# Recurrent heads: latent values and query computed as a fourth pair of half products

## The reference, cut to what matters

```
p = h @ w_in                       # q, zf, zb, i, g, b5, b6, b7, ... each 1024 wide
f = sigmoid(z); k = sigmoid(-z)    # per direction (with the zero lower bounds of one layer)
s_t = f_t * s_{t-1} + k_t v_t      # over context, then latent tokens; the other direction reversed
o_t = q_t s_t                      # only the latent tokens' outputs are used
a = rmsnorm(o_fwd + o_bwd) * silu(g)
b = p5 * conv3(p6 * p7)
```

## Time and profile before

| | |
|---|---|
| runs | 2821.94, 2821.27, 2818.16 us; median 2821.27 |
| span of the profiled execution | 2814.1 us, first to last instruction |
| TensorE busy | 2697.8 us (96%) |
| VectorE / ScalarE / GpSimd busy | 1246.7 (44%) / 523.0 (19%) / 171.2 (6%) us |
| mean granted TensorE clock | 0.987 of full speed |
| recurrent heads 1 to 7 | about 125 us to 665 us of the span |

### The profile page before, as it was taken

The page is one execution under the profiler, slowest core; times in us unless marked ns, Lnnn a source line. Parts: engine busy times, 40 slices in busy tenths (PEclk is TensorE's granted clock), DMA queues, the critical chain, the costliest instruction groups (busy, mean ns, idle before and its releaser), DMA issues.

```text
span 2814.1 us, 32083 instructions
## 1 busy us (share of the span) xinstructions
PE 2697.8 (96%) x12682; PEld 1796.7 (64%) x12682; DVE 1246.7 (44%) x2310; ACT 523.0 (19%) x870; POOL 171.2 (6%) x140
## 2 busy tenths in 40 slices
PE   7999999999899999999799999989999999999997
PEld 3688888887544444586344333334496877888886
DVE  4255656664444344535311111146573335654644
ACT  3122121222233233211100000022322113100001
POOL 1122211220000000132000000000000000000000
PEclk9999999999999999999899999999999999999999
DMA  9622111211111111225599999942102421233330
GB/s 346 212 60 57 54 52 45 60 30 38 38 53 53 45 53 49 79 75 183 231 409 409 409 409 409 409 154 64 42 1 83 125 77 46 78 87 90 90 90 30
DMA packets 327673, 374.57 MB, mean 133 GB/s; under 512 B 10033, under 2 KB 273030, under 8 KB 324230
## 3 DMA queue, kind: packets, MB, share of 16 engines
q1 hardware_dynamic: 327286, 371.93, 38.6%
q10 hardware_dynamic: 272, 1.05, 0.1%
HBM read 370.85 MB, written 2.10 MB: 133 GB/s over the span
## 4 chain that ended last, share of the span: by engine, by line
PE 91%; DVE 4%; DVEq 1%; DMA 1%; ACT 1%; issue 1%; SPq 0%; ACTq 0%
PE psum L1650 31%; PE psum L1952 12%; PE psum L1381 8%; PE psum L2108 6%; PE psum L720 3%; PE psum L1118 2%; PE psum L1837 2%; PE psum L815 2%; PE psum L728 2%; PE psum L2642 2%; PE psum L1878 2%; PE psum L705 2%; PE psum L1308 2%; PE psum L1360 2%; PE psum L1337 1%; PE psum L2724 1%
## 5 line engine op out<-in xcount | busy, mean ns | idle before, releaser
L1650 PE MATMUL psum<-arena 128*128 128x256 f32 x4144 | 907.9, 378 | 1.0 <-ACT arena L2740 0.5
L1650 PEld LDWEIGHTS psum<-arena 128*128 128x128 f32 x4144 | 779.2, 189 | 116.2 <-issue 5.3
L1952 PE MATMUL psum<-arena 128*64 128x512 f32 x1536 | 347.6, 597 | 3.0 <-issue 2.1
L1952 PEld LDWEIGHTS psum<-arena 128*64 128x64 f32 x1536 | 104.9, 136 | 217.5 <-issue 214.4
L1381 PE MATMUL psum<-arena 128*128 128x512 f32 x512 | 233.1, 597 | 0.0
L2108 PE MATMUL psum<-arena 128*128 128x512 f32 (+1 forms) x448 | 168.1, 532 | 0.0
L1682 DVE TENSOR_TENSOR arena<-psum,arena 128x256 f32<-128x256 f32 x66 | 28.0, 425 | 315.2 <-ACT arena L1695 192.6
L1381 PEld LDWEIGHTS psum<-arena 128*128 128x128 f32 x512 | 92.4, 189 | 104.1 <-issue 104.1
L1883 DVE SCALAR_TENSOR_TENSOR arena<-psum,arena 128x512 f32<-128x512 f32 x64 | 48.0, 750 | 246.4 <-PE psum L1878 245.8
L2108 PEld LDWEIGHTS psum<-arena 128*128 128x128 f32 x448 | 84.8, 190 | 80.8 <-issue 77.3
L1657 POOL TENSOR_TENSOR arena<-arena 128x512 f32<-128x512 f32 x34 | 48.2, 1418 | 1119.7 <-DMA arena<-in_w_in 653.3
(11 more groups left out here) (378 smaller groups left out, 3202.9 us busy)
## 6 DMA issues: line engine op xcount, KB each, us to landing
arena<-in_w_gate SPq DMA_DIRECT2D x64, 1024.0 KB, 18.3
arena<-in_w_up SPq DMA_DIRECT2D x64, 1024.0 KB, 16.2
arena<-in_w_down SPq DMA_DIRECT2D x64, 1024.0 KB, 18.0
arena<-in_w_in SPq DMA_DIRECT2D x120, 512.0 KB, 4.0
arena<-in_ada_w SPq DMA_DIRECT2D x24, 1024.0 KB, 7.4
arena<-in_w_up SPq DMA_DIRECT2D x32, 512.0 KB, 5.3
arena<-in_w_down SPq DMA_DIRECT2D x32, 512.0 KB, 4.8
arena<-in_w_out SPq DMA_DIRECT2D x16, 512.0 KB, 3.8
```

Of the source, the lines that this page charges most:

```text
L1650: mm = pe.matmul(psum[:, base + b, c * HALF:(c + 1) * HALF], w, v, start=(first and q == 0 and m in (0, 2, 3, 4)), stop=(last and q == KC ...
L1952: mm = pe.matmul(psum[64 * e:64 * e + 64, bank + n, :], tokens(e, 2 * q + k), w[:, k, 512 * n:512 * n + 512], start=(q == 0 and k == 0), s ...
```

## The change

Latent values and latent query become pair 3 of `pe_seven`. The values come out with channels on partitions, so TensorE turns them (four transposes) into bank 5, and ScalarE copies them straight into `hw_v`. Only the two context tiles keep the plain value product. The query stays in `hq_o` until `dve_take` has read it, and level 0 reads it there. The backward gates move behind pair 1, level 5 behind them; the values and key transposes stand ahead of pair 3; the states stand in the middle of pair 3; level 0 of the next head moves ahead of the head's norm sum. GpSimd forms four sums for a head. In head 0 the modulation parts stand elsewhere.

```diff
         def pool_hg_sums(pool, i, g):
 ...
             if g == 1 and not is_first(i):
-                done(pool, "hg", i - 1, 3)
+                done(pool, "hg", i - 1, 7)
             if g == 2:
                 if not is_first(i):
                     done(pool, "hg", i, 1)
                 pool.wait_ge(sem("head_gates"), i + 1)
+            if g == 3:
+                done(pool, "hg", i, 3)
             weight_sums(pool, *hg_pair(g), hg_sums(g), "hq_sums")
...
         def pe_hg_quad(pe, i, g, within):
-            pe.wait_ge(sem("hq_sums"), i * 3 + g)
-            pe.wait_ge(sem("hq_out"), i * 3 + g)
-            if g == 0:
-                pe.wait_ge(sem("head_query"), i)
+            pe.wait_ge(sem("hq_sums"), i * 4 + g)
+            pe.wait_ge(sem("hq_out"), i * 4 + g)
...
+        def pe_hg_gate(pe, i, d):
+            if d == 0 and not is_first(i):
+                pe.wait_ge(sem("head_out"), i)
+            ws.arrived(pe, "hg", i, 4 + d)
 ...
+            if d:
+                mm.then_inc(sem("head_gates"), 1)
...
+        def pe_turn_values(pe, i):
+            pe.wait_ge(sem("hq_out"), i * 4)
+            for t in range(LT):
+                mm = pe.transpose(psum[:, 5, t * P:(t + 1) * P], hq_o[:, t * P:(t + 1) * P], ident)
+            mm.then_inc(sem("head_turned"), 1)
...
         def dve_begin(dve, i):
-            dve.wait_ge(sem("head_query"), i)
-            dve.tensor_copy(hw_q0, hp_q)
+            dve.wait_ge(sem("head_forget"), i)
...
             pe_hg_quad(pe, 0, 1, lambda pe, q: late(6, 7) if q == 2 else None)
             late(8, 9)
-            pe_hg_values(pe, 0, 0)
-            late(10, 11)
-            pe_hg_quad(pe, 0, 2, lambda pe, q: late(12, 13) if q == 2 else None)
+            pe_hg_values(pe, 0)
+            pe_hg_quad(pe, 0, 2, lambda pe, q: late(10, 11) if q == 2 else None)
+            late(12, 13)
             late(14, 15)
-            pe_hg_values(pe, 0, 1)
-            pe_hg_query(pe, 0)
...
+            pe_hg_quad(pe, 0, 3, turn_first)
             pe_mod_turn(pe, 2)
+            pe_turn_values(pe, 1)
+            pe_level(pe, 1, 0)
...
-                pe_level(pe, i, 0)
                 pe_hg_quad(pe, i, 0, levels({3: 1}))
-                pe_hg_gates(pe, i, lambda: pe_level(pe, i, 2))
+                pe_hg_gate(pe, i, 0)
+                pe_level(pe, i, 2)
                 pe_hg_quad(pe, i, 1, levels({1: 3, 3: 4}))
+                pe_hg_gate(pe, i, 1)
                 pe_level(pe, i, 5)
-                pe_hg_values(pe, i, 0)
                 pe_hg_quad(pe, i, 2, levels({1: 6, 3: 7}))
-                pe.wait_ge(sem("head_values_out"), i * 2 + 1)
+                pe_hg_values(pe, i)
+                pe.wait_ge(sem("head_gates_out"), i + 1)
                 pe_turn_keys(pe, i)
-                pe_hg_values(pe, i, 1)
-                pe_states(pe, i)
...
-                pe_hg_query(pe, i, outputs)
+                pe_hg_quad(pe, i, 3, lambda pe, q: pe_states(pe, i) if q == 2 else None)
+                pe.wait_ge(sem("head_values_out"), i + 1)
+                pe_outputs(pe, i)
+                pe_turn_values(pe, i + 1)
+                pe_level(pe, i + 1, 0)
                 pe_head_norm(pe, i)
...
             with act.Fori(1, HEADS) as i:
                 act_hg_copy(act, i, 0)
-                act_hg_gates(act, i)
                 act_hg_copy(act, i, 1)
                 act_hg_silu(act, i)
-                act_hg_values(act, i, 0)
+                act_hg_gates(act, i)
                 act_hg_copy(act, i, 2)
+                act_hg_forget(act, i)
+                act_hg_values(act, i)
                 act_turn_keys(act, i)
-                act_hg_forget(act, i)
-                act_hg_values(act, i, 1)
+                act_hg_copy(act, i, 3)
                 act_square(act, i)
-                act_hg_query(act, i)
+                act_turn_values(act, i + 1)
...
                 dve_begin(dve, i + 1)
+                dve_hg_quad(dve, i, 3)
                 dve_readout(dve, i)
...
         def pe_tail(pe):
-            pe_level(pe, HEADS, 0)
```

More of the change, by code:

```diff
@@ L496, in dve_mod, with dve_mod_last @@
             dve.sem_inc(sem("mod_ready"), 1)
[L498 to L502, removed]
+        def dve_mod_last(dve):
             dve_mod_add(dve, 2)
@@ L613, in mixed_block_kernel @@
         hgp = Carve(arena, CT_LO, UNIT_LO)
-        hp_q = hgp.take(S)
         hp_f = hgp.take(2, T)
         hp_k = hgp.take(2, T)
-        hp_v = hgp.take(NT, P)
+        hp_v = hgp.take(CT_, P)
         hp_g = hgp.take(S)
         cv_y = hgp.take(S)
-        hw_q0 = hgp.take(S)
         hw_k0 = hgp.take(S)
@@ L636, in mixed_block_kernel @@
         hq_o = hgp.take(2 * S)
+        hp_q = hq_o[:, S:2 * S]
         hq_sums = [hgp.take(3 * 4, P).rearrange("p (m k) n -> p m k n", m=3) for _ in range(2)]
@@ L664, in pool_hg_sums @@
                 pool.wait_ge(sem("head_gates"), i + 1)
+            if g == 3:
+                done(pool, "hg", i, 3)
             weight_sums(pool, *hg_pair(g), hg_sums(g), "hq_sums")
         def pool_hg(pool):
-            for g in (1, 2):
+            for g in (1, 2, 3):
                 pool_hg_sums(pool, 0, g)
             with pool.Fori(1, HEADS) as i:
-                for g in range(3):
+                for g in range(4):
                     pool_hg_sums(pool, i, g)
@@ L694, in gates_bank @@
             return 4 if is_first(i) else 6
-        def pe_hg_gates(pe, i, between):
-            if not is_first(i):
+        def pe_hg_gate(pe, i, d):
+            if d == 0 and not is_first(i):
                 pe.wait_ge(sem("head_out"), i)
-            for d in range(2):
-                ws.arrived(pe, "hg", i, 4 + d)
+            ws.arrived(pe, "hg", i, 4 + d)
+            for k in range(KC):
+                if is_first(i) and d == 0:
+                    pe.wait_ge(sem("first_normed"), KC + k + 1)
+                mm = pe.matmul(psum[:, gates_bank(i), d * C:(d + 1) * C], ws.dst("hg", 4 + d)[:, k, :], HT[:, k, 0:C],
+                               start=(k == 0), stop=(k == KC - 1))
+            if d:
+                mm.then_inc(sem("head_gates"), 1)
@@ L702, in pe_hg_gates, with pe_hg_values @@
+        def pe_hg_values(pe, i):
+            ws.arrived(pe, "hg", i, 6)
+            for t in range(CT_):
                 for k in range(KC):
-                    if is_first(i) and d == 0:
-                        pe.wait_ge(sem("first_normed"), KC + k + 1)
-                    mm = pe.matmul(psum[:, gates_bank(i), d * C:(d + 1) * C], ws.dst("hg", 4 + d)[:, k, :], HT[:, k, 0:C],
+                    mm = pe.matmul(psum[:, 7, t * P:(t + 1) * P], HT[:, k, t * P:(t + 1) * P], ws.dst("hg", 6)[:, k, :],
@@ L706, in pe_hg_gates @@
                                    start=(k == 0), stop=(k == KC - 1))
[L707 to L731, removed]
+            mm.then_inc(sem("head_values"), 1)
+        def pe_turn_values(pe, i):
[3 more added lines that the diff above has]
+            mm.then_inc(sem("head_turned"), 1)
@@ L733, in act_hg_copy @@
         def act_hg_copy(act, i, g):
             done(act, "hg", i, 2 * g + 1)
-            if g:
+            if g == 0 and not is_first(i):
+                act.wait_ge(sem("head_taken"), i)
+            if g in (1, 2):
                 act.wait_ge(sem("hq_read"), i * 2 + g)
+            if g == 3:
+                act.wait_ge(sem("head_forget"), i + 1)
             if is_first(i) and g == 0:
@@ L746, in act_hg_gates @@
             act.wait_ge(sem("head_gates"), i + 1)
-            wait(act, sem("head_taken"), i)
             src = psum[:, gates_bank(i), :].rearrange("p (d n) -> p d n", d=2)
@@ L752, in act_hg_silu, with act_hg_values, act_turn_values @@
         def act_hg_silu(act, i):
-            act.wait_ge(sem("hq_out"), i * 3 + 2)
+            act.wait_ge(sem("hq_out"), i * 4 + 2)
             act.activation(hp_g, hq_o[:, S:2 * S], ACT.Silu)
[L756 to L762, removed]
+        def act_hg_values(act, i):
+            act.wait_ge(sem("head_values"), i + 1)
+            act.activation(hp_v, psum[:, 7, 0:C].rearrange("p (t e) -> p t e", t=CT_), ACT.Copy)\
                .then_inc(sem("head_values_out"), 1)
         def act_hg_forget(act, i):
-            act.wait_ge(sem("hq_out"), i * 3 + 3)
+            act.wait_ge(sem("hq_out"), i * 4 + 3)
             src = hq_o.rearrange("p (d n) -> p d n", d=2)
             act.activation(hp_f[:, :, C:T], src, ACT.Sigmoid)
[L769 to L773, removed]
+            act.activation(hp_k[:, :, C:T], src, ACT.Sigmoid, scale=-1.0).then_inc(sem("head_forget"), 1)
+        def act_turn_values(act, i):
+            act.wait_ge(sem("head_turned"), i)
+            act.activation(hw_v[:, CT_:NT, :], psum[:, 5, :].rearrange("p (t e) -> p t e", t=LT), ACT.Copy)\
+               .then_inc(sem("head_turned_out"), 1)
         def dve_hg_quad(dve, i, g):
-            dve.wait_ge(sem("hq_copied"), i * 3 + (g + 1))
+            dve.wait_ge(sem("hq_copied"), i * 4 + (g + 1))
```

(23 more changed lines are left out.)

15 lines of the change are left out of this document (7 added, 8 removed).

## The result

The kernel became slower: 2853.50 us, median of 4 runs (2852.53 to 2854.34), against 2820.93 for the kernel before (2818.16 to 2821.94); ratio 1.0113, 95% interval 1.0101 to 1.0125. The forecast was 2860, the range 2843 to 2879. One of the twelve runs of experiment 7 took 5736.07 us; it counts in that experiment's median and not in its ratio.

A forecast was written before the change was run, and what follows sets the result against it. TensorE, 91% of the chain of waits, was taken as the bound. The median 2821.3 plus 37 for heads 1 to 7 (3.6 + 1.7 each) plus 2 for head 0 and tail gave 2860 us, range 2843 to 2879.

The forecast's parts named there:

- Work saved: TensorE in each head: 14.03 us of latent values and query removed, 12.54 added for pair 3 and transposes; 1.5 us saved.
- The wait for pair 2's sums: Between level 5 and pair 2, TensorE waits for GpSimd's sums, which start behind the backward gates: 5.0 us a head.
- Who pays for the collision: GpSimd's sums beside VectorE on shared SBUF: GpSimd's sum slows, taken as 5.5 us, between 4.98 and 6.20.
- The clock: Behind the new wait in each looped head, TensorE runs a spell at half clock: 1.7 us, bounds 0 and 2.5.
- The rival with the clock up: Same wait ahead of pair 2, but no slow-clock spell behind it: 2848 us, chance 0.14.
- Level 3: TensorE waits there for VectorE's level 2, with the gates no longer between: about 0.6 us, bounds 0.4 and 0.9.
- Level 1: TensorE waits there for VectorE's level 0 after the next head's pair 0: 0.1 us, bounds 0 and 0.5.
- End of the head: After pair 3: turning waits 0.74 us for recombination, pair 0 starts 5.7 us after pair 3's end; waiting falls from 1.1 to 0.75.
- the table load's extra drain: ScalarE's table switch might drain about 1.38 us more, delaying level 1 by 1.4 us a head; left out of the sum.
- Head 0 and tail: Head 0, with 3 us of waiting for a modulation part's load, +1; with the tail's +1.2, together +2 us.
- Base: The 7.2 us outside the span don't change, so a difference is added to the earlier kernel's median, 2821.27 us.
- The second rival: VectorE's chain of levels also bounds, adding waits of 2 to 3 us in a head: 2878 us, chance 0.12.

The follow-up runs named there:

- experiment 7: Changed kernel with a third buffer for pair 2's sums, formed by GpSimd right behind pair 0's at the end of the head before: 2818.52 us, ratio 0.9989.
- experiment 1: Changed kernel with the backward gates ahead of pair 1 again, everything else kept: 2832.64 us, ratio 1.0033.
- experiment 2: Changed kernel, order untouched, with pair 2's fourth sum in a buffer of its own instead of over half of zb: 2825.85 us, ratio 1.0019.
- Experiment 3: Changed kernel with the context values computed once more and thrown away, between level 5 and pair 2: 2845.28 us, ratio 1.0081.
- experiment 4: Changed kernel with its own context values moved from behind pair 2 to between level 5 and pair 2: 2842.29 us, ratio 1.0070.

## Why the prediction was right

- **Work saved, 1.5 us a head.** Records at the predicted prices: pair 3 in 12.1 us besides the states (272.30 to 278.35 is its first half), turning 0.50 with level 0 behind it (208.06 to 208.56) for 0.45. Experiment 7, where nearly all waits are gone, is 77.01 - 76.57 = 0.44 us shorter than before, though by starts it waits 0.61 at level 3, 0.80 at level 6 and 0.24 at level 1, where the kernel before didn't, and 0.65 less at level 5 and the head's end. 0.44 + 1.65 - 0.65 = 1.44.
- **The wait for pair 2's sums.** Predicted 5.0 (bounds 4.5 and 5.7), measured 4.36 by starts (246.65 + 0.96 to 251.97), a little below the lower bound. Two parts were mis-sized. The sum took 4.97 us and not 5.5, though VectorE ran level 5 beside it; and the step from its end to TensorE took 0.10, not 0.25. The prediction also has pair 1's recombination beside this sum. It isn't: the recombination ends at 246.52 and the sum starts at 246.90, behind the gates. Experiments 1 and 2 take the wait away in two ways and save 21 and 28 us.
- **Who pays for the collision.** The prediction let GpSimd pay; here VectorE did. Level 5's four products (changed kernel, in order of time) took two to three times what they take elsewhere, 0.41, 0.42, 0.55 and 0.55:

```profile
248.77 0.91 DVE L837 TENSOR_TENSOR arena<-arena 128x256 f32<-128x256 f32 x1
249.60 1.31 DVE L838 TENSOR_TENSOR arena<-arena 128x256 f32<-128x256 f32 x1
250.84 1.44 DVE L839 TENSOR_TENSOR arena<-arena 128x384 f32<-128x384 f32 x1
252.21 1.66 DVE L840 TENSOR_TENSOR arena<-arena 128x384 f32<-128x384 f32 x1
```

  The rule of the Trainium skill (GPSIMD Engine Reference, 1. Specifications) names the right instructions. The recombination of pair 3, with an operand in PSUM, stands beside pair 0's sums (from 205.36 and 204.99) and kept its 0.41 to 0.69 us. That section doesn't say which side is slowed, and I charged GpSimd. In these rows the slowed one is the one that starts second. Each product starts after one of GpSimd's operations and ends 0.28 to 0.41 us behind that operation's end (249.68 behind 249.40, 250.91 behind 250.63, 252.28 behind 251.87, 253.87 behind 253.46), while GpSimd's first five operations keep their 1.09 to 1.28 us. Before the change, VectorE's operation at 225.90 was there first and kept its 0.69 us, and GpSimd's at 225.93 took 1.80; VectorE's next one came second and took 1.23 for 0.49 (kernel before, VectorE in order of time). No experiment shifts the order of such a pair by itself.

```profile
225.90 0.69 DVE L785 TENSOR_TENSOR arena<-arena 128x512 f32<-128x512 f32 x1
226.79 1.23 DVE L788 TENSOR_SCALAR arena<-arena 128x512 f32<-128x512 f32 x1 [0.19 <-issue]
```

- **The clock.** Predicted 1.7 us a head and measured 1.8 in the quarter (4.82 against 3.02), in each head. Experiment 3 shows it by itself, and that only 1.3 of it is net. The rival with the clock up would be 2848 by its own sum. The median lies about as near to that as to 2860; it is the rows at half clock in each head that put it out.
- **Level 3**: predicted 0.6, measured 0.61 by starts (3.63 from 228.48 to 232.11). **Level 1**: 0.1 predicted, 0.24 measured. **End of the head**: pair 0 starts 5.56 us after pair 3's end (5.7 predicted), the turning waits 0.6 (0.74). Level 4, states and key copies wait for nothing, as predicted, and the table load's extra drain, which the prediction left out of its sum, did not show: the logarithm starts at 210.67, the load began at 209.38 and took 1.28.
- **Head 0 and tail**: the load's wait 3.35 (3 predicted) with a slow stretch behind it, the entry wait 2.72 (2.5), together 2.4 and 1.2 us in the tail. Predicted +2, measured +3.6, of which 1.3 arose ahead of head 0's changed steps and is no part of the change.
- **Base.** The difference forecast was 39 us; by spans it is 37.7, by medians 32.6. The 7.2 us that I took for the time outside the span is 2.1; the other 5 is how far the profiled execution lay from the median. The median moved less than the trace. That 37.7 lies so near to 39 is partly luck: the wait was 7 x 0.64 = 4.5 us too long in the sum and the 1.7 us of the slow stretch at the loop's entry were not taken off, while 1.8 us in code that wasn't changed, 1.6 in head 0 and the tail, and about 1 each for level 1 and the clock stood against it.
- **The range.** Its ends were added up from 3.0 and 0.8, 5.3 and 2.4 us a head. The bounds that the prediction states give 2.8 and 0, 5.5 and 2.5, and a range of about 2841 to 2885; the measured time lies in both.
- The second rival (VectorE takes the bound as well) did not happen in this kernel: the wait of 4.3 us gave VectorE its time back, and the slow quarter hid what was left (0.44 us at level 6, experiment 3). It is what appears as soon as that wait is taken away (experiments 1 and 2). My expectation of experiment 1 failed on this step: I had counted pair 1's recombination as harmless to GpSimd's sums and had not asked what hides it from TensorE once the gates are gone.

## What to carry to other kernels

List everything that the next step waits for at each border between two steps, with the time each needs after the last one's end, and give the border work that covers the longest. A step that is moved to cover one may be what starts another: here the gates cover 3.4 us of recombination and start 5 us of sums. A dependency that exists only because a result overwrites its input was cheaper here to remove by a buffer (experiments 2 and 7) than to cover by order (experiments 1 and 4).

## What the runs showed of the hardware

- A wait of 4.3 us was followed by a slow stretch in every head, one of about 1.9 (experiment 1) or 2.25 us (experiment 4) in three heads of seven, and waits of 1.4 (experiment 2) or 0.7 us (experiment 3) in none. Work that is thrown away paid: 25 us more of it made the kernel 8 us faster.
- GpSimd and VectorE beside each other on SBUF: the loser varies, and in the rows read here it is the one that starts second. GpSimd's sum took 4.97 us beside level 5's products, which took two to three times theirs, and VectorE's copies beside GpSimd went from 0.50 to 2.50 us. Beside the convolution both paid: the sum took 6.20 us, and three of VectorE's operations took 1.23, 1.48 and 1.33 us, against 0.49, 0.75 and 0.75 after the change, where no sum stands beside them.
